# Time mixing on one Trainium2 core: the dense products of a round are dealt evenly behind the first and behind the second pair's products

## The reference, cut to what matters

```
def rwkv7_step(state, inp):
    r_t, w_t, k_t, v_t, a_t, b_t = inp
    sa = einsum('bhvk,bhk->bhv', state, a_t)
    state = state * w_t[:, :, None, :] + sa[..., None] * b_t[:, :, None, :] + v_t[..., None] * k_t[:, :, None, :]
    return state, einsum('bhvk,bhk->bhv', state, r_t)
...
    r, k, v = xr @ w_r, xk @ w_k, xv @ w_v          # 256 x 1024 by 1024 x 1024, three times
    g = sigmoid(xg @ g1) @ g2
...
    return (y.astype(h.dtype) * g) @ w_o
```

## Time and profile before

| | |
|---|---|
| median of 3 runs | 2606.65 us (2606.24 to 2608.19) |
| the profiled execution | 2605.7 us, its span 2604.2 us |
| TensorE busy, by the page | 2571.2 us, 99% of the span |
| VectorE, ScalarE, GpSimd busy | 2036.0, 1606.4 and 237.2 us |
| the four units of time mixing | about 750 to 946 us from the span's start |

### The profile page before, as it was taken

The page is one execution under the profiler, slowest core; times in us unless marked ns, Lnnn a source line. Parts: engine busy times, 40 slices in busy tenths (PEclk is TensorE's granted clock), DMA queues, the critical chain, the costliest instruction groups (busy, mean ns, idle before and its releaser), DMA issues.

```text
span 2604.2 us, 44062 instructions
## 1 busy us (share of the span) xinstructions
PE 2571.2 (99%) x17916; PEld 2225.3 (85%) x17916; DVE 2036.0 (78%) x2936; ACT 1606.4 (62%) x2362; POOL 237.2 (9%) x236
## 2 busy tenths in 40 slices
PE   8999999999999999999999999999999999999999
PEld 7999899999978879998888888888888888888887
DVE  6667676776666657668766788999999899999997
ACT  6557665554542235553555536887788878787875
POOL 1101000000111216010700200000000000000000
PEclk9999999999999999999999999999999999999999
DMA  7554355455422235553455545999999999999994
GB/s 280 181 182 146 114 184 177 175 206 181 140 88 82 67 131 178 194 209 118 166 188 187 181 152 213 368 372 352 357 359 376 353 354 370 364 371 356 365 366 163
DMA packets 85390, 609.69 MB, mean 234 GB/s; under 512 B 9608, under 2 KB 9864, under 8 KB 12224
## 3 DMA queue, kind: packets, MB, share of 16 engines
q1 hardware_dynamic: 82080, 594.58, 62.2%
q10 hardware_dynamic: 2752, 9.09, 0.9%
q0 software_dynamic: 352, 3.15, 0.3%
HBM read 605.73 MB, written 1.05 MB: 233 GB/s over the span
## 4 chain that ended last, share of the span: by engine, by line
PE 95%; DVE 3%; ACT 1%; issue 1%; DMA 0%; ACTq 0%; DVEq 0%
PE bank L439 93%; PE bank L3323 1%; DVE weights_lo L429 0%; ACT weights_hi L421 0%; DVE mean L580 0%; DMA x_T<-in_x 0%; DVE rstd L496 0%; PE bank L2192 0%; ACT squares L478 0%; DVE arena L589 0%; DVE x_T L905 0%; DVE arena L2682 0%; DVE source L663 0%; PE bank L1186 0%; DVE arena L1980 0%
## 5 line engine op out<-in xcount | busy, mean ns | idle before, releaser
L429 DVE TENSOR_TENSOR weights_lo<-raw_weights,weights_hi 128x1024 fp32r<-128x1024 f32 x816 | 1003.2, 1249 | 356.2 <-ACT weights_hi L421 351.2
L421 ACT CAST weights_hi<-raw_weights 128x1024 fp32r<-128x1024 f32 x816 | 848.7, 1051 | 299.5 <-PE bank L439 280.4
L439 PE MATMUL bank<-source,weights_hi 128*128 128x512 f32 (+1 forms) x2464 | 613.6, 365 | 13.1 <-ACT weights_hi L421 9.5
L439 PEld LDWEIGHTS bank<-source,weights_hi 128*128 128x128 f32 x2464 | 412.8, 190 | 59.8 <-ACT weights_hi L421 9.5
L439 PE MATMUL bank<-weights_hi,source 128*128 128x512 f32 (+1 forms) x1280 | 387.1, 385 | 1.5 <-DVE source L663 1.0
L439 PE MATMUL bank<-source,weights_lo 128*128 128x256 f32 x2112 | 380.4, 282 | 0.0
L439 PEld LDWEIGHTS bank<-source,weights_lo 128*128 128x128 f32 x2112 | 338.3, 190 | 37.6 <-DVE weights_lo L429 0.3
L429 DVE TENSOR_TENSOR weights_lo<-arena,weights_hi 128x1024 fp32r<-128x1024 f32 x278 | 336.1, 1224 | 30.3 <-ACT weights_hi L421 27.0
L421 ACT CAST weights_hi<-arena 128x1024 fp32r<-128x1024 f32 x278 | 292.4, 1054 | 50.7 <-PE bank L439 35.9
L439 PEld LDWEIGHTS bank<-weights_hi,source 128*128 128x128 f32 x1280 | 231.5, 188 | 45.0 <-issue 3.2
L439 PE MATMUL bank<-weights_lo,source 128*128 128x512 f32 (+1 forms) x640 | 243.4, 380 | 0.0
(11 more groups left out here) (352 smaller groups left out, 3404.0 us busy)
## 6 DMA issues: line engine op xcount, KB each, us to landing
raw_weights<-in_exp_in SPq DMA_DIRECT2D x134, 1024.0 KB, 6.0
arena<-in_exp_in SPq DMA_DIRECT2D x90, 1024.0 KB, 6.2
raw_weights<-in_exp_w SPq DMA_DIRECT2D x67, 1024.0 KB, 5.9
arena<-in_exp_w SPq DMA_DIRECT2D x45, 1024.0 KB, 6.2
raw_weights<-in_ffn_w_down SPq DMA_DIRECT2D x44, 1024.0 KB, 4.8
raw_weights<-in_ffn_w_up SPq DMA_DIRECT2D x43, 1024.0 KB, 4.8
raw_weights<-in_ffn_w_gate SPq DMA_DIRECT2D x42, 1024.0 KB, 4.8
raw_weights<-in_dense_w SPq DMA_DIRECT2D x33, 1024.0 KB, 4.8
```

What stands on the lines that cost most here:

```text
L421: k.act.copy(k.weights(j)[0], raw_half(k, j)).then_inc(k.w_hi_ready, 1)
L429: k.dve.tensor_tensor(lo, raw_half(k, j), hi.bitcast(F32), ALU.subtract).then_inc(k.w_ready, 1)
L439: return k.pe.matmul(dst, lhsT, rhs, start=start, stop=stop, skip_group_check=shared)
```

## The change

The loop over the two pairs of a round now takes dense steps after each pair. Behind the first pair stand (count + 1) // 2 of them, behind the second count // 2. Rounds 6 and 8 stay as they were. No instruction is added or removed, and only TensorE's program is reordered.

```
-            for pair in pairs:
+            for i, pair in enumerate(pairs):
                 next(pair)
+                for _ in range(0 if n in TURN_ROUNDS else (count + 1 - i) // 2):
+                    next(dense, None)
             for pair in pairs if n in TURN_ROUNDS else ():
                 next(pair)
-            for _ in range(count):
+            for _ in range(count if n in TURN_ROUNDS else 0):
                 next(dense, None)
```

## The result

The changed kernel takes 2619.81 us, the median of 8 runs from 2610.33 to 2622.65; the kernel before, beside it, 2606.7 (8 runs, 2606.24 to 2608.97). The ratio is 1.0040, with a 95% interval of 1.0028 to 1.0052: slower by 13 us in the medians. The forecast was +4.1 us with a range up to 2616.5, so it was wrong. (Of 109 later runs of the kernel before, one took 3475.74 us at a mean granted clock of 0.684, and it is left out of every comparison.)

The account below looks back on a forecast made before the run. TensorE was taken to bound the kernel, with 95% of the chain of waits. The terms 5.5 - 2.0 + 1.2 - 0.6 = +4.1 us took the median from 2606.65 to 2610.8 us, range 2606.5 to 2616.5.

Parts of the forecast that it names:

- a granted clock of 1.00 (the 2.4 GHz level): TensorE's clock read in the first and last unit of the time mixing, with TensorE busy 48.43 of 49.70 us in the first.
- Unit 3, +5.5 us: Sixteen added runs of dense steps (sections), each 0.36 us for changing array shape, less a wait of 0.25 us.
- Round 12, -0.25 us: In unit 3, a dense step would cover the second pair's "U" waiting for VectorE, saving 0.25 us.
- The estimate of 1.7 us: Unit 3's sixteen sections priced by a drain of about 128 cycles, two changes costing 0.11 us: 1.7 us.
- the rival of partly hidden changes: Unit 3: entering a section is hidden, so 16 x 0.20 = 3.2 us in place of 5.8; 2608.2 us, chance 0.13.
- Units 0 to 2, -2.0 us: Added sections on quarters would save 2.0 us over three units, by overlap; rounds 0 and 1 put at zero.
- The -0.36 of an "x" round: Round 2 of unit 0: lasts 1.44 us against 1.80 summed, since dense products begin in free quarters.
- the +0.19 of a "t" round: Round 3 of unit 0: lasts 1.99 us against 1.80 summed from pairs and dense steps.
- sections that cost 5.4 us: Units 0 to 2: half of 57 added sections cost 0.19 us, +5.4 in place of -2.0; 2618.2 us, chance 0.30.
- that win 16: Units 0 to 2: 45 sections at -0.36 us give -16.2 in place of -2.0; 2596.6 us, chance 0.07.
- The wait on VectorE, +1.2 us: Before the first pair's "U" of round 21, idle 0.52 us becomes about 0.9 in each of units 0 to 2.
- The spells of no named cause, -0.6 us: TensorE idle 1.06, 0.53 and 1.73 us inside second-pair "t" steps; half of a possible -1.3 us taken.

Follow-up runs that it names:

- unit3_look: Same edit as split_unit3 (dense steps dealt out after both pairs in unit 3 alone, against the kernel before), run for a profile: 2622.65 us.
- late3_first: Kernel before with all dense steps of rounds 12 to 24 of unit 3 behind the first pair: 2608.8 us, ratio 1.0008.
- split_unit3: Kernel before with dense steps dealt out after both pairs in unit 3 alone: 2621.01 us, ratio 1.0042.
- split_no_late3: Changed kernel's order in units 0 to 2 and in rounds 0, 1, 2 and 4 of unit 3; rounds 12 to 24 as before: 2608.76 us, ratio 1.0003.
- late3_from16: Kernel before with dense steps dealt out only in rounds 16 to 24 of unit 3: 2611.51 us, ratio 1.0013.
- late3_12to15: Kernel before with dense steps dealt out only in rounds 12 to 15 of unit 3: 2608.51 us, ratio 1.0008.
- units012_again: Kernel before with dense steps dealt out in units 0 to 2 except rounds 19 and 20, second measurement: 2605.19 us, ratio 0.9993.

## Why the prediction was wrong

**The step that failed** is in the first part: TensorE runs "at a granted clock of 1.00 (the 2.4 GHz level)", and then every price was worked out at that clock. The sum has no term for the clock, no rival moves it, and the range has no room for it. Without the fall the forecast would have held: the lower group of the changed kernel is 2608.5 to 2613.09 us in eleven executions, with 2611.4 in the middle, and 2610.8 was forecast. With it an execution loses some 7.7 us more in unit 3 (10.2 in unit3_look), and half of the executions have it (11 of 22). The median falls into one group or the other: 2619.81 in one measurement, 2612.74 in the next.

**A second step failed, and is hidden by the first.** The prediction followed VectorE's delay to the first pair's "U" of round 21 and called what comes after it covered ("in the rounds 21 to 24 three dense steps cover it"). The first pair's "y" step of round 22 now waits 0.53 us for ScalarE. Since a dense step stands in front of the second pair's "U" of round 21, ScalarE's copy of that "U" begins 0.86 us after the first pair's (784.39 to 785.25), where it was 0.33 (784.83 to 785.16). ScalarE works in order, and the copy for which "y" waits comes behind it. Round 21 is 0.46 us longer in each unit, +1.4 us, and this is so in all eight profiles with units 0 to 2 dealt out and in none of the other nine. The four units together are 5.4 us longer in the first profile where 4.1 was forecast, and this term is about the difference.

A warning of a kind was there, 3 us ahead of the stretch that I read. The earlier trace rows begins at 750.00; the row just before it reads

```profile
746.50:750.00 3.50, 3.25 (x53) 2.86 (x57) 3.47 (x11) 0.00 (x0) 3.11 (x5) 0.51 0.03 7
```

TensorE is at half clock here though busy for 3.25 of 3.50 us. It isn't the same case as unit 3: this spell comes 1.4 us after an idle spell of 1.2 us, while in unit 3, ahead of the fall in round 12, no load stood idle for more than 0.56 us. But it shows that in this kernel's own profile the clock falls, and a change that adds sixteen idle gaps of 0.33 us and makes each burst shorter should have had a rival "the clock falls in unit 3". The price of such a stretch would have been half its length at most; the spells of 3.4 us measure 1.4 to 1.7, 42 to 50%, and the long ones 43 to 45%.

What lets it fall is partly shown. In both disturbed executions with a trace it falls in round 12 of unit 3, where dense work starts again after the three rounds 9 to 11 without any. It fell only with late rounds dealt out (0 of 68 without), and neither half of them was seen to do it often. Just ahead of the fall the two profiles of the changed kernel differ in nothing that I can name: the same rounds, the same waits, [0.56 <-issue] in both; round 8 is 0.3 us longer in the one that falls, but not in unit3_look, which falls too. DMA is at its height there, with a share of 1.03 from 920 to 922 us, but it is 0.96 at the same place in late3_first, where the clock stays, and 0.03 in the row above, where it is at half. TensorE: Matmul & The Clock Gate of the Trainium skill tells, in its section on a second failure mode, that TensorE's clock swings when the engine idles briefly and often between groups of matmuls. The rows agree in kind, with 0.33 us of idle ahead of every pair's step, though they show one fall and no swinging, and no run shows that these idle times are the cause. Why one execution in two and not all stays open, and so does what ends the stretch after 17 us in one and 24 in the other.

**Unit 3, +5.5 us: right.** Measured 5.63 in the first profile, 5.6 in two more, 5.9 in split_unit3 with the 0.3 of round 8. The price of a section, 0.36, is confirmed by round 15 (+0.35), by split_no_late3 (0.34) and by late3_from16 (0.34). The estimate of 1.7 us, which took 128 cycles for a drain from the page TensorE: Matmul & The Clock Gate of the Trainium skill, step-by-step part on the drain, is refuted by the same rows, and so is the rival of partly hidden changes (2608.2).

**Round 12, -0.25 us inside that term: wrong in sign.** I took the dense step for a cover. It needs the result of `gated_vector`, which VectorE starts only behind the two sums of the inverse, and so begins 0.89 us after the first pair's "U" (921.45 to 922.34), exactly as before (920.33 to 921.22). Before, the second pair's "U" ran under that wait; now it stands behind it. Round 12 goes from 1.93 (920.32 to 922.25) to 2.50 us (921.45 to 923.95), +0.57 where 0.36 - 0.25 = 0.11 was reckoned. late3_12to15 measures it: 1.85 less the 0.30 of round 8 is 1.55 for four rounds, 1.2 expected. The parts add up: 1.02 for the three early rounds, 1.55 for 12 to 15 and 3.04 for 16 to 24 make 5.61, and the first profile has 5.63. The 0.46 that round 12 costs too much is mostly made good by the other sections, at 0.34 in place of 0.36.

**Units 0 to 2, -2.0 us: near in size, for the wrong reasons.** The three units are 0.3 us shorter together, with 1.3 us of the longer wait on VectorE and 1.4 of the new one on ScalarE in them. So all the rest, sections and idle spells, gives -0.26 - 1.26 - 1.38 = -2.9, where the terms -2.0 and -0.6 were forecast. None of it lies where the prices were taken: the rounds 2, 3, 15 and 16 of unit 0 don't change. Of the -2.9, -1.27 lies in the rounds 0 and 1, which had been put at zero, and some -0.5 in the rounds 22 to 24 (5.96 us before and 5.79 after in unit 0, 786.02 to 791.81). Against it stand +0.16 in round 2 of two units and +0.34 in round 3 of one; what is left is spread over the rounds 4 to 12, where the idle spells lie too. The -0.36 of an "x" round and the +0.19 of a "t" round were taken for the price of a section. They are the overlap of a pair's step with what comes behind it, whatever that is. I had compared rounds of unit 0 with sums put together from unit 3, where steps stand in front of others, and took the remainder for the price of the thing I was looking for. That the sum came near is luck. The rivals of sections that cost 5.4 us or that win 16 are refuted.

**The wait on VectorE, +1.2 us: right.** 0.52 became 0.94; in three units 1.6 became 2.8. By units012_again, where leaving the rounds 19 and 20 whole brings it back to 0.48, the cause is shown. New waits appeared as well, which I had named as a sign that I am wrong: the one on ScalarE's L2290, which costs what it lasts, as told above, and those on L2294, L2337 and L2323, 2.4 us together. The idle time put down to issue fell by 2.7 us in the same units, and which of these last waits cost time of their own was not separated.

**The spells of no named cause, -0.6 us: not shown either way.** Where they sit doesn't depend on the order: in all seventeen profiles one in each of the units 0 to 2 stands in front of the same-numbered weight load, 2559 and 2560 TensorE records apart (loads, matmuls and semaphore instructions), in whatever step that falls. How long they last differs between executions of one program. In front of the load the first of the earlier trace rows is 0.76 to 2.62 us in the nine profiles with units 0 to 2 as before and 0.46 to 1.13 in the four of the changed kernel; the third 1.73 to 2.27 and 0.39 to 1.80. One profile of each, which is what the prediction and the first reading had, can't price that. What ends them is in the traces' DMA records: in all 51 cases the load starts 2.18 to 2.49 us after a transfer of 16384 bytes on q8, the queue that the page of the profile calls "instruction". In the kernel before, the transfers start at 765.79, 815.40 and 864.37 us and the loads at 768.01, 817.63 and 866.71. So TensorE seems to wait there for its own instructions; this is argued from the times, and no kernel tested it. The spell of 0.53 in unit 1 is not one of the three.

## What to carry to other kernels

Before a price from a trace is multiplied, read the granted clock over the whole stage, not over the stretch that is convenient, and give its fall a chance and a price of its own wherever a change cuts long bursts of matmuls into short ones with idle time between them. On TensorE count the changes of array shape: a section of whole-array products among products on quarters costs a fixed 0.34 to 0.36 us here, while a section on quarters has no fixed price: single rounds moved by up to +0.3 us, and the rounds 0 and 1 of unit 0 together by -0.7. When one item of an engine that works in order is delayed, follow all that stands behind it, not only the next: here the second wait cost as much as the first. And a step moved forward to cover another's wait covers nothing if its own input comes later: look up what it waits for.

## What was not expected of the hardware

- The granted clock fell to 1.2 GHz for 17.1 and 23.9 us in a stretch in which TensorE was idle for 0.7 us at most at a time, in the two executions that show it; by their times, in 22 of 51, and in none of 68 with the late dense steps kept together.
- The idle time at a change of array shape is 0.33 us at 2.4 GHz and 0.65 us at 1.2 GHz.
- In units 0 to 2 TensorE's loads stand idle for 0.4 to 2.6 us once in 2560 of its records, among short matmuls and with no semaphore waited for, and go on 2.2 to 2.5 us after a transfer of 16384 bytes on the instruction queue, in 51 of 51 cases.
- Each of 15 spells of 3.4 us at 1.2 GHz in the units 0 and 1 follows an idle spell of TensorE of 1.2 to 2.6 us.
